# Decode attention moved into the prompt attention loop, its cache in 2 MB pieces through five buffers, and the slot tokens of the experts in another order

## The reference

```python
past_cmp = kv_pool[page_table, :, 0:2]           # 8 pages of 128 tokens for each decode batch
kc, vc = nsa_compress(cmp_rows, pos_w)           # softmax-weighted sums over blocks of 64
# nsa_attend, for the prompt and for the decode batches:
p_c = masked_softmax(q . kc - slope * dist)      # compressed branch; its sums rank the blocks
idx = top_k(importance, 16)                      # decode: 16 past blocks and the new one
p_s = masked_softmax(q . ks[idx] - slope * dist) # selected branch, paged keys and values
p_w = masked_softmax(q . kw - slope * dist)      # window branch, last 512 rows
o = gates[0] * p_c @ vc + gates[1] * p_s @ vs + gates[2] * p_w @ vw
return o @ w_out
# experts: score, best group, top 2 in it, then y = sum of gate * (silu(x wg) * (x wu)) wd
```

## Time and profile before

| | us |
|---|---|
| median of 3 runs | 1364.71 |
| lowest and highest | 1361.93, 1365.18 |
| the profiled execution, its own time | 1366.77 |
| its span | 1365.0 |
| PE busy | 1197.0 (88% of the span) |
| DVE, ACT, POOL busy | 491.4, 276.9, 76.6 |
| mean granted TensorE clock | 0.924 |

### The profile page before, as it was taken

The page is one execution under the profiler, slowest core; times in us unless marked ns, Lnnn a source line. Parts: engine busy times, 40 slices in busy tenths (PEclk is TensorE's granted clock), DMA queues, the critical chain, the costliest instruction groups (busy, mean ns, idle before and its releaser), DMA issues. The chain is left out here.

```text
span 1365.0 us, 15289 instructions
## 1 busy us (share of the span) xinstructions
PE 1197.0 (88%) x5341; PEld 726.6 (53%) x5341; DVE 491.4 (36%) x1461; ACT 276.9 (20%) x705; POOL 76.6 (6%) x89
## 2 busy tenths in 40 slices
PE   6997998967989998998799749987898999988978
PEld 5885555546855433443588535543356634333447
DVE  3774455972041111121427975621002401111142
ACT  1222123750041110010311015510003211101021
POOL 0000000110001000000000006610000100000000
PEclk9998898878987999999999968988899799999999
DMA  7366311961567999999459735344615599999930
GB/s 234 139 249 209 148 62 39 281 236 62 247 255 292 426 429 425 427 428 405 186 195 348 258 129 193 114 149 139 185 47 222 203 379 425 428 427 428 426 150 32
DMA packets 86043, 343.16 MB, mean 251 GB/s; under 512 B 14362, under 2 KB 52250, under 8 KB 69930
## 3 DMA queue, kind: packets, MB, share of 16 engines
q1 hardware_dynamic: 82474, 325.09, 61.6%
q0 software_dynamic: 2304, 8.39, 1.7%
q10 hardware_dynamic: 1184, 8.65, 1.6%
HBM read 327.47 MB, written 23.01 MB: 257 GB/s over the span
## 5 line engine op out<-in xcount | busy, mean ns | idle before, releaser
L861 PE MATMUL mh<-expert_ring,x_packed 128*64 128x512 f32 x768 | 180.6, 626 | 26.0 <-DMA expert_ring<-in_moe_w_up 21.9
L1105 DVE TENSOR_TENSOR hid<-mh,silu_gate 128x512 f32<-128x512 f32 x16 | 11.1, 692 | 373.4 <-PE mh L861 373.4
L861 PEld LDWEIGHTS mh<-expert_ring,x_packed 128*64 128x64 f32 x768 | 61.4, 144 | 142.9 <-issue 140.8
L179 PE MATMUL pj<-xT,expert_ring 128*128 128x264 f32 (+1 forms) x400 | 92.3, 395 | 11.2 <-DMA expert_ring<-in_ssd_w_in 11.2
L179 PEld LDWEIGHTS pj<-xT,expert_ring 128*128 128x128 f32 (+1 forms) x400 | 76.6, 192 | 26.4 <-issue 11.5
L883 PE MATMUL mo<-expert_ring,hid_T 128*64 128x512 f32 x384 | 85.0, 595 | 0.0
L367 PE MATMUL ss<-xT,expert_ring 128*128 128x264 f32 x256 | 77.6, 450 | 4.9 <-PEq L143 4.9
L596 PE MATMUL on<-conv_out,expert_ring 128*128 128x264 f32 x256 | 59.6, 398 | 10.7 <-DVE conv_out L607 10.7
L937 PE MATMUL mg<-acc,expert_ring 128*128 128x264 f32 x256 | 61.8, 407 | 7.2 <-ACT acc L646 7.2
L367 PEld LDWEIGHTS ss<-xT,expert_ring 128*128 128x128 f32 x256 | 52.5, 217 | 26.2 <-issue 16.7
L1226 PE MATMUL np<-xT,expert_ring 128*128 128x264 f32 (+1 forms) x272 | 61.2, 386 | 1.7 <-PEq L732 1.7
(11 more groups left out here) (382 smaller groups left out, 1683.5 us busy)
## 6 DMA issues: line engine op xcount, KB each, us to landing
expert_ring<-in_moe_w_gate SPq DMA_DIRECT2D x24, 2048.0 KB, 23.0
expert_ring<-in_moe_w_up SPq DMA_DIRECT2D x24, 2048.0 KB, 26.4
expert_ring<-in_moe_w_down SPq DMA_DIRECT2D x24, 2048.0 KB, 25.3
expert_ring<-in_ssd_w_in SPq DMA_DIRECT2D x10, 2048.0 KB, 8.4
expert_ring_more<-in_moe_w_gate SPq DMA_DIRECT2D x8, 2048.0 KB, 20.5
expert_ring_more<-in_moe_w_up SPq DMA_DIRECT2D x8, 2048.0 KB, 24.9
expert_ring_more<-in_moe_w_down SPq DMA_DIRECT2D x8, 2048.0 KB, 28.4
cmp_pages<-in_cmp_pages SPq DMA_DIRECT2D x64, 256.0 KB, 4.3
```

The source lines that it names most:

```text
L179: last = nc.tensor.matmul(bank[m % 8][0:M, 0:T], wc[:, k, (m % 4) * P:(m % 4) * P + M], xT[:, k, :], start=k == 0, stop=k == KD - 1)
L861: last = mm(hb[w][s * CAP:(s + 1) * CAP, :], xg[:, k, s * CAP:(s + 1) * CAP], unit(6 * i + 2 * w + s)[:, k * FF:(k + 1) * FF], start=k == ...
L1105: V.tensor_tensor(hid[:], hb[1][:], sg[:], ALU.mult).then_inc(hid_ok, 1)
```

## The change

- The two preparation blocks, the prompt loop and the decode block become one block. The input projection is followed by the loop without a barrier. The decode work stands between the steps of the prompt pairs: keys in pairs 1 to 4, window in 5 and 6, importance in 7, turned compressed values in 9 and 10, turned probabilities in 11, values in 12 to 14.
- A decode product takes four batches at once, each in a group of 32 columns of TensorE with its own 32 stationary columns (`dec_keys`, `dec_values`); before it took one batch at a time.
- The cache comes in twelve pieces j of 2 MB through five buffers (`KV_SLOT`): `ring[:, 0]` and two chunks. Pieces 0 to 3 are keys (16 pages each), 4 and 5 window keys, 6, 7, 9 and 10 values (16 pages each), 8 and 11 window values. Page numbers are read four at a time, behind the wait for the buffer.
- The compressed cache goes through `ring[:, 0]` too, three buffers of 2 MB. `tail(0)` loads batches 0 to 2 in place of expert units 2, 0 and 1 of layer 1; those units are loaded at the end of the attention block. GpSimd multiplies the odd batches, DVE the even ones; DVE sums all.
- In each expert stage the slots of pair 0 go through PE ahead of projections 2 to 7, and the slots of the other seven pairs behind `gate_up(0)`. The second gather, `turn_rows(1)` and `pack(1)` follow from there.
- Semaphores of the first layer are cleared and freed once behind it. So an order row of the new kernel shows the wait of a newer semaphore under an older name (`ld_z0` is `c_used`, `s_ld_pos` is `kv_used`).

```diff
             return 16 * (L * (7 if n % 8 < 2 else 6) + n // 8 + 1)
 
+
+        ln_sems = [sem("ln_" + n) for n in ("mean", "cent", "sq", "var", "sqrt", "norm", "out")]
...
@@ -611,8 +636,8 @@
                 for c in range(2):
                     chunk_count[c] += 2
 
+        nc.clear_and_free_semaphores(ssd_sems)
...
-                            load_unit(sp, 1, 2, unit(2))
+                            load_cmp(sp, 0)
                             sp.wait_ge(ln_sems[0], 2 * L + 2)
                             for c in range(2):
                                 load_chunk(sp, c, I["nsa_w_in"][c])
                             for c in range(2):
                                 sp.wait_ge(e_done, 4 * c + 4)
-                                load_unit(sp, 1, c, unit(c))
+                                load_cmp(sp, 1 + c)
...
-                        for m in range(2, 5):
-                            project(m)
...
                         pe.wait_ge(r_slots, 4 * L + 2)
+                        pe.wait_ge(r_xtok, 6 * L + 4)
                         slot_tokens(0, ob[0], 0).then_inc(r_idx, 1)
-                        for m in range(5, KD):
+                        for m in range(2, KD):
                             project(m)
-                        pe.wait_ge(r_slots, 4 * L + 4)
-                        for i in range(1, NP2):
-                            last = slot_tokens(i, ob[1], (i - 1) * (1 + NE))
-                        last.then_inc(r_idx, 1)
-                        pe.wait_ge(r_over, L + 1)
+                        def other_slots():
+                            pe.wait_ge(r_slots, 4 * L + 4)
+                            for i in range(1, NP2):
+                                last = slot_tokens(i, ob[1], (i - 1) * (1 + NE))
+                            last.then_inc(r_idx, 1)
...
+                            else:
+                                other_slots()
                             turn(i)
-                            if i + 1 < NP2:
+                            if 1 <= i < NP2 - 1:
                                 turn_rows(i + 1)
                             down(i)
+                            if i == 0:
+                                turn_rows(1)
...
+                            if i == 0:
+                                pack(1)
...
+            KV_SLOT = (1, 2, 0, 3, 4, 1, 2, 0, 3, 1, 2, 0)
...
+            def load_kv(sp, j):
+                s = KV_SLOT[j]
+                for g in range(4):
+                    if j < 4:
+                        b, table, first = 2 * g + j % 2, "ksel_pages", 4 * (j // 2)
+                    elif j < 6:
...
+                    else:
+                        b, table, first = 2 * g + (j - 6) // 3, "vsel_pages", 4 * ((j - 6) % 3)
+                    pages = [page_number(sp, b * NPG + first + q) for q in range(4)]
+                    for q in range(4):
+                        src = I[table][bass.ds(pages[q], 1)].rearrange("a p c -> (a p) c")
+                        sp.dma_start(kv_buf[s][:, (4 * g + q) * 256:(4 * g + q + 1) * 256], src).then_inc(ld_kv[s], 16)
...
+                    for b in range(3, DB):
+                        sp.wait_ge(c_used, b - 2)
+                        load_cmp(sp, b)
+                    for j in range(3):
+                        sp.wait_ge(c_used, 6 + j)
+                        load_kv(sp, j)
+                    sp.wait_ge(tile_done, d0 + 20)
+                    load_kv(sp, 3)
+                    sp.wait_ge(tile_done, d0 + 21)
+                    load_kv(sp, 4)
...
+                    for j in range(5, 9):
+                        sp.wait_ge(kv_used, j - 4)
+                        load_kv(sp, j)
+                    for j in range(9, 12):
+                        sp.wait_ge(kv_used, j - 3)
+                        load_kv(sp, j)
+                    load_chunk(sp, 1, I["nsa_w_out"][1])
+                    sp.wait_ge(kv_used, 9)
+                    load_chunk(sp, 0, I["nsa_w_out"][0])
+                    for n in (1, 2, 0):
+                        sp.wait_ge(kv_used, 12 if n == 0 else 9 + n)
+                        load_unit(sp, 1, n, kv_buf[n])
+
...
+                    for b in range(1, DB, 2):
+                        pool.wait_ge(ld_cmp[cmp_slot(b)], 16 * NPG * (b // 3 + 1))
+                        for a in range(4):
+                            x = cmp_buffer(b)[:, :, a, :].rearrange("p n (c l) -> p n c l", l=BLK)
+                            i1 = nc.gpsimd.tensor_tensor(x, x, wb[:, a:a + 1, :].unsqueeze(1).to_broadcast([P, NPG, 2, BLK]), ALU.mult)
+                        i1.then_inc(c_mult, 1)
...
+                    def dec_keys(j):
+                        t, a, s = j % 2, j // 2, KV_SLOT[j]
...
+                        pe.wait_ge(ld_kv[s], kv_landed(j))
+                        k5 = kv_buf[s].rearrange("p (g q c t) -> p g q c t", g=4, q=4, c=2)
+                        for p in range(2):
+                            for g in range(4):
+                                q0 = (2 * g + t) * P + 32 * g
+                                last = mm(dp[a][32 * g:32 * g + 32, :], qbd[:, p, q0:q0 + 32], k5[:, g, :, p, :], start=t == 0 and p == 0, stop=t == 1 and p == 1)
+                        last.then_inc(kv_used, 1)
+
...
+                        v4 = kv_buf[s].rearrange("p (g q c) -> p g q c", g=4, q=4)
+                        for q in range(4):
+                            for g in range(4):
+                                last = mm(o[g], ptd[:, 4 * r + q, 32 * g:32 * g + 32], v4[:, g, q, :], start=False, stop=r == 2 and q == 3, skip_group_check=True)
+                        last.then_inc(kv_used, 1)
...
+                    for pair in range(NU // 2):
+                        if pair + 2 < NU // 2:
+                            score(pair + 2)
...
+                        if 1 <= pair <= 4:
+                            dec_keys(pair - 1)
+                        if 5 <= pair <= 6:
+                            dec_window(pair - 1)
+                        if pair == 7:
+                            dec_importance()
+                        if 9 <= pair <= 10:
+                            turn_cmp_values(2 * pair - 18)
+                        if pair == 11:
+                            turn_probs(0)
+                            turn_probs(1)
+                        turn(2 * pair)
+                        if pair == 4:
+                            dec_small()
+                        if 9 <= pair <= 10:
+                            turn_cmp_values(2 * pair - 17)
+                        if pair == 11:
+                            turn_probs(2)
+                            turn_small()
+                        if 12 <= pair <= 14:
+                            dec_values(2 * pair - 18)
+                        if pair >= 1:
+                            values(pair - 1)
+                        if 12 <= pair <= 14:
+                            dec_values(2 * pair - 17)
+                        turn(2 * pair + 1)
...
+                    def compress(b):
+                        x4 = [cmp_buffer(b)[:, :, a, :].rearrange("p n (c l) -> p n c l", l=BLK) for a in range(4)]
+                        if b % 2 == 0:
+                            dve.wait_ge(ld_cmp[cmp_slot(b)], 16 * NPG * (b // 3 + 1))
                             for a in range(4):
-                                x = cpg[:, b % 2, :, a, :].rearrange("p n (c l) -> p n c l", l=BLK)
...
```

More of the change, by code:

```diff
@@ L612, in trunk @@
                     chunk_count[c] += 2
-        ln_sems = [sem("ln_" + n) for n in ("mean", "cent", "sq", "var", "sqrt", "norm", "out")]
+        nc.clear_and_free_semaphores(ssd_sems)
         class Norm:
@@ L665, in trunk @@
         CAP = 64
-        router_sems = [sem("r_" + n) for n in ("log", "sig", "turn", "gate", "rank", "slots", "xtr", "xtok", "idx", "tok", "rows", "got", "over", "row0", "row1")]
-        ple_sems = [sem("e_" + n) for n in ("ld", "done", "sig", "out", "proj", "pre")]
-        moe_sems = [sem("m_" + n) for n in ("gather", "packed", "gate_up", "silu", "hid", "turned", "ht", "down", "ys", "scatter", "acc")]
         def tail(L, out=None):
@@ L718, in tail @@
                 sc_bank = [ob[0], gb[0], ob[1], gb[1]]
[L719 removed]
+                o_ld, o_dve, o_pe, o_act = over_sems[L]
                 NPE, NDV = 1 + NF + KD, 1 + 2 * NF + KD
@@ L1709, in trunk @@
+            for c in range(2):
+                chunk_count[c] += 1
         tail(1, out=O["y"])
```

996 lines of the change are left out of this document (500 added, 496 removed).

## The result

The changed kernel takes 1289.9 us (median of 4 runs, 1285.3 to 1301.6), the one before 1365.0 beside it (1361.9 to 1374.2): a ratio of 0.945, 95% interval 0.937 to 0.953. Six more runs on another chip gave 1291.1 (1287.9 to 1292.6), ratio 0.946 (0.943 to 0.948). The forecast was 1278, within 1262 to 1300. The profiled execution took 1286.8, its span is 1285.0, against 1277.0 in the forecast's sum.

What follows compares the result with a forecast made beforehand. SP's issue of cache pages was taken to bound the attention block, weight transfers the expert stages. 1365.0 + 7.3 (seam) + 0.7 (clearing) - 90 (attention) - 6 (experts) = 1277.0 span; forecast 1278 us, range 1262 to 1300.

Steps and rivals of the forecast that it cites:

- SP sets the pace: Attention block from 54 us on: SP's page loads, 1.10 us a page and 17.5 for 16, bound it.
- rival 3: Attention: register loads overlap page loads, so the engines bind, 189 us rather than 247: 1220; chance 0.07.
- none of the waits ahead of them binds: Attention: SP's last issues, until 200, are not delayed by waits; 20 us left ahead of piece 10.
- rival 4: SP's queue: each register load takes 995 ns rather than 266, giving 1371, or 1400 with compressed pages; chance 0.03.
- Key piece 0 at 54: Attention: key pages start 54 us into the block, after batch 7's issue from 46; 49 without any wait of SP.
- rival 1: Attention start: DVE and POOL multiplications block each other, piece 0 at 64, end 10 us later, 1288; chance 0.2.
- The short row that I weighed against rival 1: Evidence against blocking: a 0.16 us DVE product, two elements per partition, ran inside POOL's 0.92; called thin proof.
- The seam, +7.3: Ahead of the attention: eight pages of batch 2 read and issued, 8.6 us, so PE starts at 708.1, not 700.8.
- Clearing the semaphores, 0.7: One more meeting of the engines; a seam costs 0.3 to 2 us, taken as 0.7.
- The end of the block, 47 us behind the last issue: Attention: last issue at 200, block end at 247, with the output weights landing at 213 and just hidden.
- The expert stages, -3 each: Each of two layers: 9.8 us earlier start, less 5.4 standing and 1.5 restart, gains 3; -6 in all.
- from the first issue at 8.8 four units last until 28.4; the stream stands for 5.4: Expert stages: four queued weight units end before units 12 and 13 issue at 33.8, so the stream stands 5.4 us.

Runs made afterwards that it cites:

- e10_changed_again: The changed kernel run once more, unaltered, on another chip: 1291.1 us.
- e1_slots_only: The kernel before with only the new order of the slot tokens, the attention being the old one: 1355.7 us against 1366.2 before.
- e2_fixed_pages: The changed kernel with key and value page numbers from constants, without 128 register loads, not computing what the reference asks: 1253.8 us.
- e11_other_buffer: Changed kernel with DVE alone multiplying, early page-number reads, ACT issuing some key and value pages and output weights, value piece 10 in the fifth buffer: 1244.4 us.
- e9_attention_only: The changed kernel with the old order of the slot tokens, so the new attention alone: 1303.6 us.
- e5_reads_ahead: The changed kernel with page numbers read ahead of each wait of SP rather than behind it: 1281.8 us.
- e3_dve_alone: The changed kernel with DVE multiplying all eight batches and POOL none: 1285.1 us.
- e6_act_shares: The changed kernel with ACT issuing the second half of key pieces 0, 1 and 3 (24 key pages): 1270.6 us.

## Why the prediction was right, and where not

**SP sets the pace: right for the stretch, wrong for its end.** 17.6 us for 16 pages stood against 17.5 forecast, PE waited for pages in pairs 3, 4 and 14, and taking the reads away gained 36 us, so rival 3 (SP not the bound) is out. But the step "none of the waits ahead of them binds" failed: SP stood 2.3 us ahead of piece 10, for pair 12, where I had left 20 us of slack. In the second profile of the changed kernel, with its key pages 2.4 us later, it didn't stand there: the wait is just at its edge. Pairs with decode work take about 6 us, not the 4.8 that I reckoned with: PE's 1.9 for a piece stands on top of the 3.6 of a bare pair, and one step of DVE holds PE for 5.4 (869.00 above). What isn't pages took 13 us where I had 6. That is +7, or +7.5 with half a microsecond of the pages' own: windows and store 8.5, that wait, 0.6 of another, and five register loads that were slow behind the store and the second window piece:

```profile
L117 SPq TENSOR_LOAD <-page_table x5: 273/610/899, 838.6 to 844.7; - x5
```

So rival 4 (slow register loads) exists, but only for a handful of reads: 1.9 us here, and a median of 266 ns over all 192.

**Key piece 0 at 54: it came at 65**, +11. By the rows it has three parts. The first is rival 1: the lock doubled DVE's first four products, 4.3 us on the path of the sum for which batch 3 waits. The second is batch 3's landing: issued from 717.5, multiplied from 730.1, 12.6 us where I had counted 8.3, by a median landing. A 2 MB piece of weights went out at 716.1, and 4 MB at 390 GB/s is 10.8 us:

```profile
718.00:723.00 5.00, 5.00 (x25) 4.25 (x24) 4.97 (x5) 0.39 (x1) 0.00 (x0) 1.00 0.93 389
723.00:727.00 4.00, 4.00 (x20) 3.42 (x19) 3.63 (x4) 0.66 (x2) 0.00 (x0) 1.00 1.03 387
```

The weights piece as the cause is supported by the runs in which batch 3 was issued 4.3 to 4.4 us sooner and landed only 0.2 to 2.3 sooner; moving the weights wasn't tried. Ahead of the prediction I gave 47 to 258 GB/s for the slices of the old attention, and overlooked one of 348, from 717 to 751: beside the projection the transfers were not idle before either. The third part is 2 us of issuing: three of batch 6's eight page loads took 1.17 to 1.39 us on SP rather than 0.33, and the batch 10.8 rather than 8.7 (744.1 to 754.9). Why is not shown. The parts hide each other: taking the lock away moved the first key page by 2.9 us and not by 4.3.

The rival's price was too high. It let each of DVE's four products wait for one of POOL's, 9.4 us in all, and only two of the four met one (3.37 us rather than 1.22, twice 2.15). What the second meeting costs changes between executions. In the profile above DVE's four products of batch 4 were through in 4.62 us, and POOL lost 2.1 at 746.36. In the second profile of the changed kernel, `e10_changed_again`, DVE was held again, the block was 2.1 us longer, and the first key page went 2.4 later (69.7 of the block):

```profile
744.23 8.92 DVE L1594 TENSOR_TENSOR expert_ring<-expert_ring,pos_softmax 128x1024 f32<-128x1024 f32 x4
```

So 1288 of rival 1 is near the measured time, but for less than half the reason.

The lock is as the traces show it: 4.6 us become 8.94 on DVE and 9.3 become 12.29 on POOL. The short row that I weighed against rival 1 outweighed nothing: products of 1024 elements for each partition do block. Why that one, of two elements, ran through is not shown.

**The seam, +7.3: right**, 8.97 against 1.69. At four seams of the kernel before PE stood 0.79, 1.69, 1.14 and 0.79 us (at 376.5, 700.8, 1008.7 and 1038.2). Clearing the semaphores, 0.7, is not to be seen. It stands at another seam, ahead of the first expert stage, and PE waits 0.79 us there with the clearing (the changed kernel) and without it (`e1_slots_only`).

**The end of the block, 47 us behind the last issue: right** (47.6), with 2.7 for the output weights not hidden and 30.1 for their products. The 247 has 1 us for the seam ahead of these products, where PE stood 1.14 before and stands 2.68 now, and 2 for a slow clock at their start, which no run shows: they take 1.4 more than the 28.72 of before, at a granted clock of 0.66 in their first 4.2 us and 1.00 behind. In `e2_fixed_pages`, at 1.00 throughout, they took 28.72. Column groups do run at once. In the kernel before, at a granted clock of 1.00, products of 512 columns in two groups of 64 took 0.43 us each, and those of 256 columns, one after the other, 0.45. In four groups of 32, 16 value products took 1.93 us at 1.00, 0.12 each (`e11_other_buffer`, above), so the low end of my range, 1.8, was the true one.

**The expert stages, -3 each: measured -6.9 and -6.5.** The step that failed is "from the first issue at 8.8 four units last until 28.4; the stream stands for 5.4". Units 6 and 7 wait for the last projection. Its end stays at 410.5 while gate_up(0) moves to 412.1 from 423.8, so they now go out just ahead of units 8 to 11. Six units were queued, and nothing stood. The old stream had stood there for most of 10 us, which the prediction didn't count as something to be won back. Its 1.5 for a restart the kernel before does show: from the issue at 432.38 to 435.00 its transfers ran at 181 GB/s and then at 426, so 1.5 of 2.6 us were lost. The changed kernel has no such restart there. `e1_slots_only` and `e9_attention_only` give 10.5 and 12.5 for both stages.

The sum: +11.0 for piece 0, +7.5 for windows and waits, +0.2 at the end, -7.4 in the expert stages, -0.7 for the clearing and -2.5 ahead of it all: +8, from 1277.0 to 1285.0. The time came within 1% in part by luck, because errors of 19 and 11 us went against each other. The forecast of 1278 also isn't what its own last step gives: 1277.0 with 1.8 added and 2.1 taken off is 1276.7.

## What to carry to other kernels

Where one queue sets the pace, list for every wait on it what frees the buffer, and what pace that consumer has once the queue is relieved: removing 73 us of issue gave 36, and a later 9 us gave nothing until one buffer was changed. What a wait doesn't guard, such as reading a page number, belongs ahead of it (8 to 9 us in `e5_reads_ahead`). Where a stream might stand, count the units that are queued by then from their issues, and count those whose issue the change moves. Where a load starts beside a large one, an estimate from bytes and rate, 10.8 us here, is nearer than the median: batch 3 took 12.6 where 8.3 was counted.

## What the runs showed of the hardware

The lock also takes copies. Four DVE copies of 64x32 elements from SBUF to SBUF took 6.00 us in all beside POOL's products, up to 2.3 each, and 0.18 each with POOL idle. The first line is the changed kernel's, the second that of `e3_dve_alone`:

```profile
L1612 DVE COPY expert_ring<-q_T x4: 183/1736/2299, 771.5 to 777.3; 64x32 f32<-64x32 f32 x4
```
```profile
L1612 DVE COPY expert_ring<-q_T x4: 171/182/186, 769.2 to 769.8; 64x32 f32<-64x32 f32 x4
```

A register load on ACT's queue took 276 ns at the median, on SP's 266, and 8.8 us of reads and issues in one lot beside the projection didn't hold PE (its 336 records run without a gap in `e6_act_shares`, from 699.05 to 777.07):

```profile
699.05 78.02 PE L1318 MATMUL na<-xT,expert_ring 128*128 128x264 f32 x336 [8.97 <-PEq L754]
```
